# Hymba decoder step on one core: x and one parameter row loaded first, DT and the first GLU pairs computed quarter by quarter of K as x's tiles come

## The reference

```python
u = rmsnorm(x, norm_pre_mix)                 # x: 320 tokens x 2048
proj = u @ w_in                              # 2048 x (2048 z + 3072 xbc + 32 dt + 4096 glu)
dt = softplus(dt_raw + dt_bias)              # 32 heads; cum = cumsum(dt * A) for the scan
v = glu[..., :2048] * sigmoid(glu[..., 2048:])
vc, new_conf_buf = causal_depthwise_conv(v, conf_buf, conf_conv_w, conf_conv_b)   # 31 taps, state of 30 rows
# then: the SSD scan with z and xbc, W_out, RMSNorm and residual, an MLP of 8192, RMSNorm and residual
```

## Time and profile before

| | us |
|---|---|
| median of 3 runs | 2021.49 (2021.17 to 2024.51) |
| the profiled execution's own time | 2020.32 |
| its span, first to last instruction | 2018.7 |
| PE busy | 1847.4 (92%) |
| DVE / ACT / POOL busy | 1151.7 / 727.3 / 490.6 |
| DMA | 278.72 MB, mean 138 GB/s |

### The profile page before, as it was taken

How to read it: one execution, slowest core, us unless ns; L and a number is a source line. 1 busy time by engine, 2 the same in 40 slices (tenths; PEclk the granted TensorE clock), 3 DMA queues, 4 the chain that set the end, 5 groups by cost and what they waited for, 6 DMA issues and landing times.

```text
span 2018.7 us, 34917 instructions
## 1 busy us (share of the span) xinstructions
PE 1847.4 (92%) x12467; PEld 1799.1 (89%) x12467; DVE 1151.7 (57%) x1992; ACT 727.3 (36%) x1019; POOL 490.6 (24%) x378
## 2 busy tenths in 40 slices
PE   0999999999996999986965999999999999999995
PEld 0799999999995888866965999999999999999995
DVE  0678777999876556547558443344433444344454
ACT  1543334444436333323313333343333433234331
POOL 1157676666651111111233000000000000000131
PEclk9999999999997999997987999999999999999998
DMA  5445554444452444443521444444445454444541
GB/s 154 157 127 149 147 160 140 130 148 138 144 151 81 137 130 140 136 144 107 162 84 57 152 150 146 163 132 160 155 138 159 132 165 151 141 154 137 166 145 52
DMA packets 286391, 278.72 MB, mean 138 GB/s; under 512 B 9355, under 2 KB 283787, under 8 KB 285410
## 3 DMA queue, kind: packets, MB, share of 16 engines
q1 hardware_dynamic: 247472, 246.97, 40.3%
q10 hardware_dynamic: 37206, 23.45, 3.8%
q0 software_dynamic: 1648, 7.43, 1.2%
HBM read 262.03 MB, written 17.22 MB: 138 GB/s over the span
## 4 chain that ended last, share of the span: by engine, by line
PE 80%; DVE 10%; issue 3%; DMA 3%; ACT 2%; DVEq 1%; POOL 1%; ACTq 0%; POOLq 0%; SPq 0%
PE ps L1503 24%; PE ps L1505 24%; PE ps L1504 24%; DMA dsk<-in_d_skip 2%; DVE ps L1182 2%; PE ps L1743 1%; PE ps L1752 1%; PE ps L1718 1%; DVE wlo L1039 1%; DVE ps L1221 1%; DVE alo L1417 1%; PE ps L1697 1%; DVE mix L1411 0%; DVE sqs L1279 0%; DVE gss L1374 0%
## 5 line engine op out<-in xcount | busy, mean ns | idle before, releaser
L1503 PE MATMUL ps<-ahi,whi 128*128 128x320 f32 x2704 | 848.8, 314 | 53.8 <-DVE alo L1381 17.9
L1504 PE MATMUL ps<-alo,whi 128*128 128x320 f32 x2704 | 840.8, 311 | 0.0
L1505 PE MATMUL ps<-ahi,wlo 128*128 128x320 f32 x2704 | 840.7, 311 | 0.0
L609 ACT ACTIVATE whi<-raw 128x1024 fp32r<-128x1024 f32 (+1 forms) x468 | 481.1, 1051 | 568.0 <-PE ps L1505 451.9
L1039 DVE TENSOR_TENSOR wlo<-raw,whi 128x1024 fp32r<-128x1024 f32 (+1 forms) x345 | 448.6, 1326 | 258.1 <-ACT whi L609 252.7
L1503 PEld LDWEIGHTS ps<-ahi,whi 128*128 128x128 f32 x2704 | 512.9, 190 | 59.0 <-issue 32.3
L1504 PEld LDWEIGHTS ps<-alo,whi 128*128 128x128 f32 x2704 | 513.0, 190 | 0.5 <-issue 0.2
L1505 PEld LDWEIGHTS ps<-ahi,wlo 128*128 128x128 f32 x2704 | 512.5, 190 | 0.0
L435 POOL TENSOR_TENSOR wlo<-raw,whi 128x1024 fp32r<-128x1024 f32 x123 | 298.8, 2453 | 115.2 <-ACT whi L609 115.0
L1503 PE MATMUL ps<-hhi,whi 128*128 128x320 f32 x1024 | 316.4, 309 | 0.0
L1504 PE MATMUL ps<-hlo,whi 128*128 128x320 f32 x1024 | 316.4, 309 | 0.0
(11 more groups left out here) (257 smaller groups left out, 1150.9 us busy)
## 6 DMA issues: line engine op xcount, KB each, us to landing
raw<-in_w_in SPq DMA_DIRECT2D x144, 512.0 KB, 3.7
raw<-in_w_up SPq DMA_DIRECT2D x128, 512.0 KB, 4.4
raw<-in_w_down SPq DMA_DIRECT2D x128, 512.0 KB, 4.6
raw<-in_w_out SPq DMA_DIRECT2D x64, 512.0 KB, 3.6
h<-in_state_ssm ACTq DMA_DIRECT2D x16, 512.0 KB, 5.0
out<-hout ACTq DMA_DIRECT2D x16, 512.0 KB, 3.0
x_transposed<-xt ACTq DMA_DIRECT2D x1, 2560.0 KB, 8.8
xr<-x_transposed POOLq DMA_DIRECT2D x1, 2560.0 KB, 9.2
```

The lines of the kernel that those rows point to most:

```text
L609: act.activation(whi[:, kq, :, 0:width], raw[:, kq, :, 0:width], ACT.Copy).then_inc(hi_done, 1)
L1503: pe.matmul(out, wh, hi[:, kk, :], start=(kk == 0), stop=False)
L1504: pe.matmul(out, wh, lo[:, kk, :], start=False, stop=False)
L1505: last = pe.matmul(out, wl, hi[:, kk, :], start=False, stop=(kk == NT - 1))
```

## The change

SP's first twelve weight loads are now in the order DT, GLU gate, GLU value for each quarter of K, in slots `s % 4`. POOL issues its state DMAs only when x has landed. ACT's queue starts with one extra row, `norm_pre_mix`, into `prow0`; PE turns it at once and ACT copies it to `pmx`, which scales the tiles in place of `par`. All other parameter rows are turned by PE between the third and the fourth quarter, and copied by ACT after `glu(0)`'s last splits. The 16 tiles of x are worked in four groups of four; after each group come three splits (DT, gate, value of that quarter), and PE runs their 60 matmuls and turns four more tiles of x, now through 3 PSUM banks. `glu(0)` as a loop body is gone; the states are turned within `glu(1)`. DVE runs `dt_part(0)` to `(2)`, `make_v(0)`, `dt_part(3)` to `(6)`, and then `glu(1)`.

```diff
-            for kq in range(4):
-                load(in_k[:, 4 * kq:4 * kq + 4, COL_DT:COL_DT + P], Q_DT, kq, P)
+            for s in range(12):
+                kq, m = s // 3, s % 3
+                col, width = ((COL_DT, P), (COL_GLU + D, 256), (COL_GLU, 256))[m]
+                if s >= 4:
+                    sp.wait_ge(lo_done[s % 4], s // 4)
+                sp.dma_start(raw[:, s % 4, :, 0:width], in_k[:, 4 * kq:4 * kq + 4, col:col + width]
+                             ).then_inc(raw_ready[s % 4], 16)
 
...
+            pool.wait_ge(x_in[2], 16)
...
-                for c in range(1, 6):
+                for c in range(6 if first else 1, 6):
                     split(Q_GLU, i, c)
...
+            glu(1)
...
+            act.dma_start(prow0[:], norm_pre_mix).then_inc(pmx_in, 16)
             act.dma_start(prow[R_CONV:R_CONV + TAPS, :], conf_conv_w[0]).then_inc(par_in, 16)
...
+            expect_root()
+            act.wait_ge(pmx_trans, 1)
+            act.activation(pmx[:], ps[:, 4, 480:480 + NT], ACT.Copy).then_inc(pmx_done, 1)
...
-            act.activation(sw[:, 0:NT, :], par[:, :, R_XW:R_XB + 1], ACT.Copy).then_inc(par_done, 1)
+            def keep_x(t):
+                act.wait_ge(x_trans, t + 1)
+                act.activation(xt0[:, t, :], ps[:, 5 + t % 3, 0:TOK], ACT.Copy).then_inc(x_copied, 1)
+
+            def first_split(s):
+                split(s // 4, s % 4, P if s % 3 == 0 else 256)
...
+            act.wait_ge(pmx_done, 1)
+            for g in range(4):
+                for t in range(4 * g, 4 * g + 4):
+                    for u in ((t,) if t % 4 == 0 and t else ()) + ((t + 1,) if t % 4 < 3 else ()):
+                        if u >= 2:
+                            keep_x(u)
+                    act.wait_ge(t1_done, t + 1)
+                    act.activation(ahi[:, t, :], t1[:, t % 2, :], ACT.Copy, scale=pmx[:, t:t + 1]
+                                   ).then_inc(ahi_done, 1)
+                if g == 3:
+                    act.wait_ge(x_copied, NT)
+                    act.dma_start(xt_dram.rearrange("p (t n) -> p t n", t=NT), xt0[:]).then_inc(xt_stored, 16)
+                for m in range(3):
+                    first_split(3 * g + m)
...
-                    act.wait_ge(weights_used, 4)
+                    act.wait_ge(weights_used, 10)
...
-                act.wait_ge(weights_used, 4 * (Q_GLU + 2 * i) + 4)
+                act.wait_ge(weights_used, 11 if isinstance(i, int) and i == 0 else 4 * (Q_GLU + 2 * i) + 4)
...
+                    if c == 0:
                         act.wait_ge(read_dve, i)
                         conv_begin(i - 1)
-                    if isinstance(i, int) and i == 0:
-                        dt_part(c)
+                    if second:
                         conv_states(c)
...
+                    if c == (7 if second else 5):
...
-            glu(0)
-            with act.Fori(1, 8) as i:
+            ahead(Q_GLU, 0, 6)
+            ahead(Q_GLU, 0, 7)
+            act.wait_ge(par_trans, 1)
...
+            act.activation(sw[:, 0:NT, :], par[:, :, R_XW:R_XB + 1], ACT.Copy).then_inc(par_done, 1)
+            dt_part(0)
+            dt_part(1)
+            sigmoid(0)
+            dt_part(3)
+            act.wait_ge(par_done, 1)
+            glu(1)
...
-            dve.wait_ge(dsk_in, 16)
-            dve.tensor_copy(prow[R_DSKIP:R_DSKIP + 1, :].rearrange("a (h p) -> a h p", p=HD),
-                            dsk[:].unsqueeze(2).to_broadcast([1, HEADS, HD])).then_inc(dsk_done, 1)
...
-            split(Q_DT, 0, P)
-            split(Q_DT, 1, P)
...
+            dve.wait_ge(pmx_done, 1)
+            for g in range(4):
+                for t in range(4 * g, 4 * g + 4):
+                    dve.wait_ge(x_copied, t + 1)
+                    if t >= 2:
+                        dve.wait_ge(act_ready, t - 1)
+                    dve.tensor_tensor(t1[:, t % 2, :], ps[:, 5 + t % 3, 0:TOK], rb[:], ALU.mult
+                                      ).then_inc(t1_done, 1)
+                    if t % 4:
+                        in_lo(t - 1)
+                in_lo(4 * g + 3)
+                for m in range(3):
+                    split((3 * g + m) // 4, (3 * g + m) % 4, P if m == 0 else 256)
+            dve.wait_ge(dsk_in, 16)
+            dve.tensor_copy(prow[R_DSKIP:R_DSKIP + 1, :].rearrange("a (h p) -> a h p", p=HD),
+                            dsk[:].unsqueeze(2).to_broadcast([1, HEADS, HD])).then_inc(dsk_done, 1)
...
-                    if isinstance(i, int) and i == 0:
-                        dt_part(c)
-                        if c == 7:
-                            dve.wait_ge(halo_zero, 1)
-                            dve.wait_ge(cst_done, NT)
-                    else:
-                        conv(i - 1, c)
+                    conv(i - 1, c)
...
-            glu(0)
-            with dve.Fori(1, 8) as i:
-                st.enter(i, 1, CONV_STEPS)
+            for c in range(3):
+                dt_part(c)
+            make_v(0)
+            for c in range(3, 7):
+                dt_part(c)
+            dve.wait_ge(par_done, 1)
+            dve.wait_ge(halo_zero, 1)
+            dve.wait_ge(cst_done, 2)
+            glu(1)
+            dve.wait_ge(cst_done, NT)
+            with dve.Fori(2, 8) as i:
+                st.enter(i, 2, CONV_STEPS)
                 glu(i)
-                st.leave(7)
...
-            pe.wait_ge(par_in, 16 * 13)
-            pe.wait_ge(dsk_done, 1)
+            pe.wait_ge(pmx_in, 16)
             for t in range(NT):
-                pe.transpose(ps[:, 5 + t // 8, (t % 8) * NROW:(t % 8 + 1) * NROW], prow[:, t * P:(t + 1) * P],
...
+                if t >= 3:
+                    pe.wait_ge(x_copied, t - 2)
+                    pe.wait_ge(t1_done, t - 2)
+                b = 5 + t % 3
...
+            def first_piece(s):
+                kq, m, slot = s // 3, s % 3, s % 4
+                bank, tiles = ((4, 1), (0, 2), (2, 2))[m]
+                pe.wait_ge(lo_done[slot], s // 4 + 1)
+                for n in range(tiles):
...
+            for t in range(3, 8):
                 turn_x(t)
+            pe.wait_ge(rb_done, 1)
+            for kq in range(4):
+                pe.wait_ge(act_ready, 4 * kq + 4)
+                for m in range(3):
+                    first_piece(3 * kq + m)
+                if kq < 2:
+                    for t in range(8 + 4 * kq, 12 + 4 * kq):
+                        turn_x(t)
+                if kq == 2:
+                    pe.wait_ge(par_in, 16 * 13)
+                    pe.wait_ge(dsk_done, 1)
+                    pe.wait_ge(x_copied, NT)
...
+                    last.then_inc(par_trans, 1)
...
-                pe.wait_ge(par_done, 1)
+                pe.wait_ge(dt_act, 1)
...
+                        if second:
                             turn_conv_states(c)
...
+                            if c in (2, 4):
+                                turn_xconv_states(c // 2 - 1)
+                        if c == (6 if second else 4):
                             turn_v(i - 1)
...
-            glu(0)
-            with pe.Fori(1, 8) as i:
+            glu(1)
+            with pe.Fori(2, 8) as i:
                 glu(i)
+            turn_dt()
```

More of the change, by code:

```diff
@@ L194, in build @@
         diag = place("diag", [P, 3, P], at=own + 648)
+        pmx = place("pmx", [P, NT], at=own + 1032)
+        prow0 = place("prow0", [1, D], at=2 * NT * TOK + 4096 * 2 + 2048)
         dsk = place("dsk", [1, HEADS], at=sm)
@@ L642, in _ @@
-            act.wait_ge(par_copied, 1)
-            act.activation(sw[:, 0:NT, :], par[:, :, R_XW:R_XB + 1], ACT.Copy).then_inc(par_done, 1)
+            def keep_x(t):
[3 more added lines that the diff above has]
+                split(s // 4, s % 4, P if s % 3 == 0 else 256)
+            for t in range(2):
+                keep_x(t)
             act.wait_ge(rb_mm, 1)
@@ L722, in glu @@
             def glu(i):
+                second = isinstance(i, int) and i == 1
                 for c in range(8):
                     ahead(Q_GLU, i, c)
-                    if c == 0 and not (isinstance(i, int) and i == 0):
+                    if c == 0:
                         act.wait_ge(read_dve, i)
                         conv_begin(i - 1)
-                    if isinstance(i, int) and i == 0:
-                        dt_part(c)
+                    if second:
                         conv_states(c)
@@ L734, in glu @@
                         sigmoid(i)
-                    if c == 5 and not (isinstance(i, int) and i == 0):
+                    if c == (7 if second else 5):
                         v_rows(i - 1)
-            glu(0)
-            with act.Fori(1, 8) as i:
+            ahead(Q_GLU, 0, 6)
+            ahead(Q_GLU, 0, 7)
+            act.wait_ge(par_trans, 1)
+            act.activation(par[:, 0:8, :], ps[:, 5, 0:8 * NROW].rearrange("p (t r) -> p t r", t=8), ACT.Copy)
+            act.activation(par[:, 8:16, :], ps[:, 6, 0:8 * NROW].rearrange("p (t r) -> p t r", t=8), ACT.Copy)
```

(22 more changed lines are left out.)

89 lines of the change are left out of this document (29 added, 60 removed).

## The result

| | before | changed |
|---|---|---|
| median of 4 runs, us | 2022.64 (2021.17 to 2024.51) | 2037.69 (2036.12 to 2038.93) |
| ratio | | 1.0074, 95% interval 1.0056 to 1.0091 |
| span of the profiled execution | 2018.7 | 2034.9 |
| mean granted clock | 0.973 | 0.965 |

I had forecast 2019.2, and 2009 to 2026.5 as the range.

The account below looks back on a forecast made before the run. PE was taken as the bound, busy 92%, with gains only where it stands still. Load at 48 plus 42.4 + 1.4 + 27.9 + 27.1 ends glu(1) at 146.8 against 149.0, 2.2 us less: 2019.2, range 2009 to 2026.5.

Parts of the forecast that it names:

- The late engine has the same work, so the gate's first load lands at 48: Start: one backlogged DMA engine, never idle, ends as before at 46.6 us; with additions the gate's weights land at 48.
- From the load to the first matmul, 5.1 us: First quarter: gate split on ACT, DVE's steps and PE's turn of tile 7 take 5.1 us after the load.
- The gaps between quarters, 2.5: Between quarters PE turns four tiles of x, taking 2.5 us warm or 3.6 cold.
- K, quarter 3's start: Start of the last quarter's matmuls, after the parameter rows are turned: L + 42.4, plus 1.4 for a clock fall.
- L: Time the gate's first weight load lands: 48 us, bounds 44 to 51.
- The dt chain, 23.1 us: From ACT's hw through DVE's dt parts to its split of glu(1)'s third granule: 23.1 us, against 31.8 before.
- 146.8: Forecast end of glu(1) on PE in us, L + 98.8 with L = 48, against 149.0 before.
- From there both kernels do the same: After glu(1) ends on PE both kernels run alike, so comparing those ends gives the whole difference, 2.2 us less.
- Rivals: the clock falls in each gap: Three more PE clock falls, before quarters 1, 2 and in glu(1)'s first granules, cost 7.5 us: 2026.7; chance 0.18.
- Rivals: the backlog clears sooner: Start: the late engine's rows pass faster or weights don't wait, load at 37 to 43, time 2008 to 2014; chance 0.30.
- loads go at their rate: Start: loads run at full DMA rate, so ACT's squares and the tiles set it; 25 us less, 1994; chance 0.06.
- The change doesn't do what it says: x early is worth nothing while the weights wait: Start: early x gains nothing since the weights wait on the same engine; no gain, counted in the forecast (0.42).

Follow-up runs that it names:

- e1: Changed kernel with POOL's store_v(0) issued behind its splits 6 and 7 in glu(1) instead of ahead: 2028.6 us, 1.0035 of the kernel before.
- e2: Changed kernel with 64 more wait instructions on PE, which do no work and move the rest of its program: 2030.6 us, 1.0042 of before.
- e3: Kernel before with 168 more wait instructions at the start of PE's program, doing no work: 2033.6 us, ratio 1.0048.
- e12: Changed kernel without POOL's wait for x, so state rows are issued at once: 2038.5 us, 1.0079 of the kernel before.
- e9: Kernel before with only POOL's wait for x's last chunk added ahead of the state DMAs: 2010.5 us, ratio 0.9945.
- e10: Kernel before with the state DMAs behind x and the 31 conf_conv_w rows loaded as 16 + 15: 1995.9 us, ratio 0.9872.
- e4: Changed kernel with the 31 conf_conv_w rows loaded by DMAs of 16 and 15 rows: 2025.2 us, 1.0012 of the kernel before.
- e7: Changed kernel with later store_v(0), 16 + 15 rows, PE's program moved, and dt parts 5 and 6 moved into glu(1): 2002.1 us, 0.9896 of before.

## Why the prediction was wrong

- **"The late engine has the same work, so the gate's first load lands at 48":** right, 46.7. x landed at 18.4, not 22.
- **From the load to the first matmul, 5.1 us:** 5.1. **The gaps between quarters, 2.5:** 2.3 both times. **K, quarter 3's start:** 86.3, where L + 42.4 + 1.4 is 91.8. Of the 5.5 us, 1.3 is the load, 1.4 a fall of the clock that did not come there, 1.0 the parameter rows (turned in 1.8 us, not 2.8), 0.8 the first quarter (9 slow matmuls and not 17), and 1.0 small waits and gaps counted too long.
- **The dt chain, 23.1 us:** 28.3, from `hw` at 90.5 to the third granule at 118.8. I had taken off all that DVE's steps lost beside POOL's splits, though two of these splits remain. Three copies of `cum` took 4.81 us beside them, and three of `ecum`, with POOL idle, 0.73. PE stands 5.0 + 9.4 us for it where I had 11. This error and that of K cancel, so it is luck that 146.8 met 146.4.

```profile
109.53 4.80 POOL L444 TENSOR_TENSOR wlo<-raw,whi 128x1024 fp32r<-128x1024 f32 x2 [6.07 <-ACT whi L619]
109.87 4.81 DVE L1174 COPY cum<-hb 32x320 bf16<-32x320 bf16 x3
```

- **"From there both kernels do the same": this step failed**, and with it the choice to compare the ends of `glu(1)`. It is false in two ways, which make 14.2 of the 18.9 us lost behind `make_v(1)`. First, the diff moves `turn_v(0)` from PE's fifth to its seventh granule of `glu(1)`, and `v_rows(0)` on ACT from c = 5 to c = 7. POOL's program still has `store_v(0)` ahead of its splits 6 and 7, which are the first granules of `glu(2)`. I had counted `turn_v` as 0.3 us of PE, and not asked what is queued behind its reader's reader: 8.1 us (e1). Second, the changed program of PE is longer, as `glu(1)` stands outside the loop, and the loop of the last quarters comes to lie where jumping back fetches instructions again: 6.1 us (e2, e3).
- **"Rivals: the clock falls in each gap":** not in the gaps between quarters. It fell once for 17 us around the dt stall, once behind POOL's stall, and shortly in places behind 390 us where both kernels have the same gap. That these short falls make some 5 us of the difference is read from the two traces; why one execution has them and another not stays open, and no run was made for it.
- **"Rivals: the backlog clears sooner" and "loads go at their rate":** neither came in the changed kernel; the gate's load landed at 46.7, not at 37 to 43 or before. The sum of 2.0 us plus the bytes at 436 GB/s is what the Trainium skill, "DMA: Bandwidth & Descriptors" (Anatomy of one DMA), gives for a DMA that POOL issues; x and the weights are issued by SP, so it was applied beyond what the page states.
- **"The change doesn't do what it says: x early is worth nothing while the weights wait":** right for the changed kernel (e12). But the reason that I gave, an engine never idle, led me to think so of x first in general, and e9 shows 12 us.
- **What quartering buys.** From the first weight matmul to `make_v(1)` is 78.2, 78.5 and 78.7 us in before, e9 and e10, and 94.6 and 95.1 in the changed kernel and e4. With nearly the same transfers, quarters start PE's weights 7.6 us sooner (e9 against changed) or 4.1 (e10 against e4), and cost 16 us after it. Of these, 10.9 are longer waits of PE in `glu(1)`, nearly all behind the dt chain (5.0 + 9.4 + 0.3, against 3.8 in `glu(0)` before). The rest is about what PE takes to turn tiles and rows between the quarters (2.3 + 2.3 + 2.0). e7 gets that down to 88, still behind.

## What to carry to other kernels

When a step is moved on one engine, follow its result to the last engine that waits for it, and look at what that engine has queued behind the wait: a store in front of two splits cost more than the prologue had won. Try the cheapest part of a change alone before the large one; here one wait on another queue and a 31-row DMA cut in two give 1.3%, and the new order of work, as it is built here and with nearly the same transfers, only takes from it. When a program gets longer, compare the instruction queue's rows at the jumps of its large loops.

## What I had not expected of the hardware

- A loop body on PE of some 1560 instructions (768 matmuls, each with its weight load, and the waits) runs its second turn without a fetch when it lies at one place in the program, and with nine fetches of 16 KB at another: 5.5 to 6.1 us, with the clock fall that follows. The rows of the profile for the queue, in the changed kernel and in e2, whose PE program is 64 instructions longer:

```profile
q8 instruction: 52, 0.85, 0.2%
```

```profile
q8 instruction: 43, 0.70, 0.1%
```

- A 512 KB split on DVE took 6.28 us while POOL ran splits and copies, 1.23 otherwise (e1). The Trainium skill, "SBUF — State Buffer" (SBUF: two separate sides), says that the two engines exclude each other from a shared port pair, for a DVE instruction with two SBUF inputs against one of POOL that reads SBUF, and that the one that starts first has it for its whole instruction. The trace agrees that one is held up. It does not agree on which: DVE's split starts at 148.58, POOL's first at 149.10, and DVE's still lasts until two splits and a copy of POOL are all but done (154.9).
- 31 rows of 8 KB in one DMA held up other queues' transfers by some 20 us: with 16 + 15 rows the gate's load was there by 27 us and not at 46.7.
